# Seven of twelve modulation slabs moved from TensorE to VectorE dot products, and the layer loop written out on three engines

## The chip, the core and the metric

The kernel runs on one core of one Trainium2 chip. The metric is the device time of one execution in microseconds (us): the median over the runs shown, lower is better. All times inside an execution are microseconds from the start of the span that the profile shows.

## What is computed

Two layers of a hybrid backbone over 384 tokens (256 latent, 128 context) of width 1024, all in float32. The change touches the modulation vectors `mod` and nothing else of the mathematics:

```python
def _layer(x, cond, prm, ctx):
    mod = jax.nn.silu(cond) @ w_mod + b_mod             # w_mod (1024, 6144), two rows of cond
    sh1, sc1, g1, sh2, sc2, g2 = [m[:, None, :] for m in jnp.split(mod, 6, axis=-1)]
    h = _rmsnorm(x, g_mix) * (1 + sc1) + sh1
    ... = _project(h, w_in, ...)                        # four mixers and four sigmoid gates
    x = x + g1 * (jnp.sum(gates * proj, axis=2) @ w_o)
    h2 = _rmsnorm(x, g_ffn) * (1 + sc2) + sh2
    a, b = jnp.split(h2 @ w_gu, 2, axis=-1)
    x = x + g2 * ((jax.nn.silu(a) * b) @ w_down)
```

`mod` has 6144 columns: 24 slabs of 256, or 48 chunks of 128. The kernel holds it as `modc`, 48 columns by two rows of `cond` (latent and context).

## The kernel before

**Units.** All big products are cut into units of 128 output columns by 384 tokens. A unit has K steps of 128 rows (8, or 4 for a `proj` unit, 5 or 6 for `down`), and a step is three matmuls (`product`, L763 to L765), since both operands are split in a high and a low part. So a K=8 unit is 24 matmuls and a K=4 unit 12. A slot of a unit on ScalarE (`slot`, then `split`) copies the high part of the weights of the unit three places on (`w_hi`, L1078, LOOKAHEAD = 3); VectorE subtracts for the low part (`w_lo`, L1329). TensorE waits for `lo_ready` of its unit. The raw weights come from SyncE's queue into a ring of four slabs (two units each).

**Order.** Nothing is scheduled at run time: `plan()` writes a table `HOOKS` that says after which unit each small step runs, and every engine walks the same table. One layer is: norm, q, k, v units; conv and pool units with attention woven in; 32 gate and proj units of the first two branches; then the stage of this change, 32 more units from N_AC on (four times four `gate` units of K=8 and four `proj` units of K=4), numbered here slot 0 to 31; then 8 `out` units from N_O on, of which the first three run as `three_units`, which first waits for `lo_ready` of all three; then norm 2, 44 feed-forward units (an inner hardware loop of four turns over 8 units, `pe.Fori(0, 4)`), and 32 `down` units.

**A proj slot on VectorE** is: low part of the unit three on, then the hooks, then the product with the gate (`gate_t`, L1377, waits for the unit's end). GpSimd adds the product into `merged` (L1773), ScalarE and VectorE split `merged` into `br_hi` and `br_lo` for the out units.

**Modulation.** Slabs of layer 0: eight at the start; slabs 8 to 19 in the 32 slots of the stage of this change (`mod` after slots 2, 4, ... 12 and 18, 20, ... 28); slabs 20 to 23 ("late") before norm 2. Each of the twelve is three hooks: `load` (ScalarE's queue, 1 MB into `mod_w`), `mod` (TensorE, eight matmuls of 256 columns, `mod_matmul` L834, then a copy of the sums by ScalarE), `sel` (TensorE, two transposes, `mod_turn` L840, then two small VectorE instructions, `mod_columns`). Layer 1 gets its columns another way: during layer 0's feed-forward and down units `dot_next` makes 34 chunks as VectorE dot products (two instructions of 128x1024 elements per chunk, L1440, one per row of `cond`, and after every second chunk one small combination, L1447); three slabs ("tail") and four late ones stay on TensorE.

**The layer loop.** `with pe.Fori(0, DEPTH) as l` (L988), and the same on the four other engines, is a hardware loop: the code of a layer stands once and a backward branch repeats it. Everything that only layer 0 does stands in `engine.If(l < DEPTH - 1)`.

Of the kernel before, what the change touches and what calls it, by code (L numbers as in the profile page):

```python
# [26 lines left out]
P = 128  # L27
# [6 lines left out]
DEPTH = 2  # L34
D = 1024
# [77 lines left out]
DOTS = 34  # L113
AHEAD = ("load", "mod", "sel", "cond_next", "load_next", "dot_next", "load_tail_next")

NA = 20
# [10 lines left out]
def plan():  # L128
# [123 lines left out]
    return units, slab_of, hooks, mid, base, last_unit  # L252

UNITS, SLABS, HOOKS, MID, BASE, LAST_UNIT = plan()
# [76 lines left out]
def program(nc, io, sizes):  # L332
    with ExitStack() as ctx:
# [134 lines left out]
        mod_in = [signal(f"mod_in{s}", 0, step=32) for s in range(2)]  # L468
# [169 lines left out]
        def mod_index(i, it):  # L638

            return i + it * 6  # L640

# [6 lines left out]
        def run_hooks(engine, l, n, it, hook, takes, mid):  # L648

            hooks = mid + HOOKS[n]
            for what, i in hooks:
# [102 lines left out]
        def _(pe):  # L755
# [93 lines left out]
            def hook(l, what, i, it):  # L849
                if what == "mod":  # L850
                    f, slot = mod_index(i, it), i % 2
                    pe.wait_ge(*mod_in[slot](0, i // 2 + it * 3))
                    if i >= 2:
                        pe.wait_ge(*mod_ready(0, f - 2))
                    mod_matmul(sc[:, slot, :], mod_w[:, slot, :], mod_sum.sem)
                elif what == "sel":
                    pe.wait_ge(*mod_row_ready(0, mod_index(i, it)))
# [130 lines left out]
            with pe.Fori(0, DEPTH) as l:  # L988
# [53 lines left out]
                with pe.If(l < DEPTH - 1):  # L1042
# [27 lines left out]
        def _(act):  # L1070
# [74 lines left out]
            def hook(l, what, i, it):  # L1145
                if what == "load":
                    f, slot = mod_index(i, it), i % 2
                    if i < 2:
                        act.wait_ge(*attn_ready(l, NA - 1))
                    if i >= 2:  # L1150
                        act.wait_ge(*mod_sum(0, f - 2))
                    load_mod(act, mod_w[:, slot, :], l, bass.ds(8 + i + it * 6, 1), mod_in[slot].sem)
                elif what == "load_late":
                    act.wait_ge(*unit_done(l, N_O - 1))
                    load_mod(act, late_w[i], l, slice(20 + i, 21 + i), late_in[i].sem)
                elif what == "mod":
                    f = mod_index(i, it)
                    act.wait_ge(*mod_sum(0, f))
                    if i >= 2:
                        act.wait_ge(*mod_col(0, f - 2))  # L1160
# [5 lines left out]
                elif what == "load_next":  # L1166

                    j = i + it * 4
                    if i >= 2:
                        act.wait_ge(*dot_both(0, j - 2))  # L1170
# [76 lines left out]
            def slot(l, n, it=0, per=0):  # L1247

                if n + LOOKAHEAD >= U:
                    with act.If(l < DEPTH - 1):  # L1250
# [3 lines left out]
                run_hooks(act, l, n, it, hook, ("load", "mod", "cond_next", "load_next", "load_tail_next"), MID[n])  # L1254
                post(l, n, it, per)
# [30 lines left out]
            with act.Fori(0, DEPTH) as l:  # L1286
# [21 lines left out]
                with act.If(l < DEPTH - 1):  # L1308
# [12 lines left out]
        def _(dve):  # L1321
# [103 lines left out]
            def hook(l, what, i, it):  # L1425
                if what == "sel":
                    dve.wait_ge(*mod_col(0, mod_index(i, it)))
                    c = 16 + 2 * i + it * 12
                    mod_columns(bass.ds(c, 2), sc[:, i % 2, :], i % 2, vec[:, bass.ds(c, 2)],
                                mod_added(0, mod_index(i, it)), mod_ready.sem)  # L1430
                elif what == "dot_next":
                    j = i + it * 4
                    if i == 0:
                        dve.wait_ge(*cond_in(0, 0))
                    dve.wait_ge(*dot_in[i % 2](0, i // 2 + it * 2))
                    if i % 2 == 0:
                        dve.wait_ge(*dot_ready(0, i // 2 + it * 2 - 1))
# [6 lines left out]
                    if i % 2:  # L1444
                        c = bass.ds(j - 1, 2) if i < 4 else slice(i - 1, i + 1)
                        b = vec_all[:, bass.ds((l + 1) % DEPTH, 1), c].rearrange("p a v -> p (a v)")
# [117 lines left out]
            def norm(l, which, start=None):  # L1564
# [30 lines left out]
                if which:  # L1595
                    dve.wait_ge(*mod_ready(0, 11))
                    gains(0, DC, tail_ready(l, -1), 4)
                for d in range(DC + 1):
                    if which == 0 and d % 2 == 0 and d < DC:
# [4 lines left out]
                        gains(d, 2, start_ready(0, d + 1) if start else dot_ready(0, DOTS // 2 - 1), d // 2)  # L1604
# [9 lines left out]
            def slot(l, n, it=0, per=0):  # L1614
# [4 lines left out]
                if n + LOOKAHEAD >= U:  # L1619
                    with dve.If(l < DEPTH - 1):  # L1620
# [3 lines left out]
                run_hooks(dve, l, n, it, hook, ("sel", "dot_next"), MID[n])  # L1624
# [58 lines left out]
            with dve.Fori(0, DEPTH) as l:  # L1683
                chain.enter("layer", l)
# [25 lines left out]
                with dve.If(l < DEPTH - 1):  # L1710
# [8 lines left out]
                chain.leave(DEPTH)  # L1719
# [134 lines left out]
```

## Time and profile before

| what | value |
|---|---|
| median of 3 runs | 1471.04 us (1470.63 to 1473.37) |
| profiled execution, own time | 1470.59 us |
| its span | 1468.8 us |
| PE busy | 1435.2 us (98%) |
| DVE busy | 873.0 us (59%) |
| ACT busy | 591.6 us (40%) |
| POOL busy | 179.0 us (12%) |
| HBM read | 211.98 MB, 146 GB/s over the span |

PE is TensorE, PEld its weight loads, DVE VectorE, ACT ScalarE, POOL GpSimd. The own time is 1.79 us more than the span. A matmul's duration is longer than the distance to the next one, since they are pipelined; costs on TensorE are read from start to start.

### The profile page before, as it was taken

Reading aid. Unit: us, or ns where it says so; the run is one execution under the profiler, and the core shown is the slowest. Engines: PE = TensorE matmul, PEld = TensorE weight load, DVE = VectorE, ACT = ScalarE, POOL = GpSimd, SP = SyncE. Lnnn points to the kernel's source line nnn. Section 1 sums busy time; section 2 is a strip of 40 time slices with the busy share of each in tenths; the row PEclk is TensorE's granted clock in tenths of the full one; section 3 lists DMA queues with packets and bytes.
Section 4 is the critical chain, followed back from the end, with each engine's and each line's share of the span. In section 5 each row is a group of like instructions: output and inputs, shape, how many; then the busy total and the mean of one; then the engine's idle time right before and its main releaser. Section 6 shows DMA issues by size and latency. Waiting matters only on the chain.

```text
span 1468.8 us, 25970 instructions
## 1 busy us (share of the span) xinstructions
PE 1435.2 (98%) x9053; PEld 1376.1 (94%) x9053; DVE 873.0 (59%) x1609; ACT 591.6 (40%) x1082; POOL 179.0 (12%) x173
## 2 busy tenths in 40 slices
PE   5999999999999999999999999999999999999998
PEld 4899999998989999999988999999999989999998
DVE  4776666553454877777876766655444574545333
ACT  3544545442343533332344544554333353333322
POOL 2220020111222000000102211101131300000000
PEclk7999999999999999999999999999999999999999
DMA  9532123346566555546844321232343733433341
GB/s 346 189 122 88 58 87 96 107 154 234 193 224 229 194 179 190 195 157 212 282 139 131 122 87 58 93 110 87 108 151 117 257 105 127 142 114 101 107 133 49
DMA packets 68371, 215.69 MB, mean 147 GB/s; under 512 B 7896, under 2 KB 9240, under 8 KB 68120
## 3 DMA queue, kind: packets, MB, share of 16 engines
q1 hardware_dynamic: 55736, 168.50, 34.2%
q10 hardware_dynamic: 12096, 44.57, 8.7%
q8 instruction: 69, 1.13, 0.3%
q0 software_dynamic: 416, 1.05, 0.2%
q14 instruction: 54, 0.44, 0.1%
HBM read 211.98 MB, written 2.11 MB: 146 GB/s over the span
## 4 chain that ended last, share of the span: by engine, by line
PE 93%; DVE 2%; issue 2%; DMA 1%; ACT 1%; POOL 0%; ACTq 0%; DVEq 0%; POOLq 0%
PE bank L763 29%; PE bank L764 28%; PE bank L765 28%; PE tr L932 2%; PE sc L908 2%; PE tr L917 2%; DMA mod_w<-in_w_mod_pack 1%; PE sc L834 1%; PE tr L864 1%; DMA tok<-in_x_prompt 0%; DVE w_lo L1329 0%; DVE nx L1581 0%; PE bank L941 0%; ACT h_hi L1241 0%; PE bank L834 0%
## 5 line engine op out<-in xcount | busy, mean ns | idle before, releaser
L763 PE MATMUL bank<-h_hi,w_lo 128*128 128x384 f32 x1664 | 568.6, 342 | 10.2 <-DVE h_lo L1334 7.6
L765 PE MATMUL bank<-h_hi,w_hi 128*128 128x384 f32 x1664 | 558.1, 335 | 0.0
L764 PE MATMUL bank<-h_lo,w_hi 128*128 128x384 f32 x1664 | 558.1, 335 | 0.0
L1329 DVE TENSOR_TENSOR w_lo<-raw,w_hi 128x1024 fp32r<-128x1024 f32 (+3 forms) x352 | 384.0, 1092 | 284.0 <-ACT w_hi L1078 283.8
L1078 ACT CAST w_hi<-raw 128x1024 fp32r<-128x1024 f32 (+3 forms) x352 | 323.6, 922 | 126.2 <-PE bank L765 104.1
L763 PEld LDWEIGHTS bank<-h_hi,w_lo 128*128 128x128 f32 x1664 | 313.8, 189 | 22.9 <-issue 15.2
L764 PEld LDWEIGHTS bank<-h_lo,w_hi 128*128 128x128 f32 x1664 | 314.1, 189 | 0.0
L765 PEld LDWEIGHTS bank<-h_hi,w_hi 128*128 128x128 f32 x1664 | 313.8, 189 | 0.0
L763 PE MATMUL bank<-br_hi,w_lo 128*128 128x384 f32 x384 | 131.9, 343 | 1.5 <-DVE w_lo L1329 1.5
L765 PE MATMUL bank<-br_hi,w_hi 128*128 128x384 f32 x384 | 128.6, 335 | 0.0
L764 PE MATMUL bank<-br_lo,w_hi 128*128 128x384 f32 x384 | 128.4, 334 | 0.0
L765 PE MATMUL bank<-f_hi,w_hi 128*128 128x384 f32 x352 | 117.6, 334 | 0.0
L763 PE MATMUL bank<-f_hi,w_lo 128*128 128x384 f32 x352 | 117.6, 334 | 0.0
L764 PE MATMUL bank<-f_lo,w_hi 128*128 128x384 f32 x352 | 117.6, 334 | 0.0
L1773 POOL TENSOR_TENSOR merged<-merged,gate_t 128x384 f32<-128x384 f32 x48 | 69.6, 1458 | 385.8 <-DVE gate_t L1377 385.8
L1201 ACT ACTIVATE prob<-sc,st,q_rs 128x384 f32<-128x384 f32 (+1 forms) x96 | 56.6, 596 | 100.5 <-DVE st L1520 50.3
L1440 DVE SCALAR_TENSOR_TENSOR unread<-mod_t,cond_all 128x1024 bf16<-128x1024 f32 x68 | 85.3, 1254 | 1.2
L763 PEld LDWEIGHTS bank<-br_hi,w_lo 128*128 128x128 f32 x384 | 72.1, 188 | 6.8 <-issue 6.8
L1090 ACT ACTIVATE f_hi<-ff_f 128x384 f32 (+1 forms) x44 | 23.1, 526 | 137.0 <-DVE ff_f L1361 137.0
L764 PEld LDWEIGHTS bank<-br_lo,w_hi 128*128 128x128 f32 x384 | 72.2, 188 | 0.0
L765 PEld LDWEIGHTS bank<-br_hi,w_hi 128*128 128x128 f32 x384 | 72.1, 188 | 0.0
L763 PEld LDWEIGHTS bank<-f_hi,w_lo 128*128 128x128 f32 x352 | 66.1, 188 | 0.0
(191 smaller groups left out, 1295.2 us busy)
## 6 DMA issues: line engine op xcount, KB each, us to landing
raw<-in_w_pack SPq DMA_DIRECT2D x224, 512.0 KB, 4.5
mod_t<-in_w_mod_t ACTq DMA_DIRECT2D x34, 512.0 KB, 3.8
raw<-in_w_pack SPq DMA_DIRECT2D x64, 256.0 KB, 3.3
mod_w<-in_w_mod_pack ACTq DMA_DIRECT2D x32, 512.0 KB, 5.0
raw<-in_w_pack SPq DMA_DIRECT2D x32, 384.0 KB, 4.0
raw<-in_w_pack SPq DMA_DIRECT2D x32, 320.0 KB, 3.5
start_w<-in_w_mod_pack SPq DMA_DIRECT2D x12, 512.0 KB, 12.8
late_w<-in_w_mod_pack ACTq DMA_DIRECT2D x8, 512.0 KB, 12.1
```

What stands on the lines that cost most here:

```text
L763: pe.matmul(out, w[1], r[0], start=start, stop=False)
L764: pe.matmul(out, w[0], r[1], start=False, stop=False)
L765: return pe.matmul(out, w[0], r[0], start=False, stop=stop)
L908: ins = pe.matmul(sc[:, g, nk * n:nk * n + nk], q_[a, 4 * m + c, P * t:P * t + P], k_[a, ks], start=r == 0, stop=r == 2)
L917: ins = pe.transpose(tr[:, g, P * b:P * b + P], prob[:, i % 2, g, P * b:P * b + P], ident)
L932: ins = pe.matmul(tr[64 * g:64 * g + 64, 0, to], vals[:, m, v, 64 * g:64 * g + 64], prob_t[:, i % 2, g, b + n, :], start=b == 0, stop=v == ...
L1078: act.copy(to, src).then_inc(hi_ready.sem, 1)
L1090: act.mul(f_hi[:, c, :].rearrange("p a t -> p (a t)"), ff_f[:, i % 2, :], 0.5).then_inc(ff_hi.sem, 1)
L1201: ins = act.activation(prob[:, i % 2, g, nk * n:nk * n + nk], sc[:, g, nk * n:nk * n + nk], ACT.Exp, scale=q_rs[:, 2 + 4 * m + c, r:r + 1] ...
L1329: dve.tensor_tensor(to, src, hi.bitcast(F32), ALU.subtract).then_inc(lo_ready.sem, 1)
L1440: dve.scalar_tensor_tensor(unread[:, :], mod_t[:, i % 2, :], 1.0, cond_all[:, c, :], ALU.mult, ALU.mult, accum_out=dot_sums[:, i % 2, c:c ...
L1773: pool.tensor_tensor(m, m, gate_t[:, d % 4, :], ALU.add).then_inc(merge_done.sem, 1)
```

## The change

In layer 0's stage from N_AC on, slabs 8 to 12 stay on TensorE (each now through the single buffer `tail_w`, `load` at slot 6x, `mod` at 6x + 4, `sel` at 6x + 5), and slabs 13 to 19 become 14 chunks that VectorE computes as dot products, at slots 3, 5, ... 29 (`dot_gate`). Their weights come as 512 KB chunks (`load_gate`), after one load of the condition rows to all partitions (`cond_gate`, 1 MB). TensorE, ScalarE and VectorE run the two layers as written-out code; the inner feed-forward loops, and the layer loops of SyncE and GpSimd, stay.

```diff
-AHEAD = ("load", "mod", "sel", "cond_next", "load_next", "dot_next", "load_tail_next")
+GATE_SLABS, GATE_DOTS = 5, 14
+AHEAD = ("cond_gate", "load_gate", "dot_gate", "load", "mod", "sel", "cond_next", "load_next", "dot_next", "load_tail_next")
...
-    for x, at in enumerate((2, 4, 6, 8, 10, 12)):
-        hooks[AC + at - 2].insert(0, ("load", x))
-        hooks[AC + at].append(("mod", x))
-        hooks[AC + at + 1].insert(0, ("sel", x))
+    gate_stage(0, "cond_gate", 0)
+    for x in range(2):
+        gate_stage(0, "load_gate", x)
+    for x in range(GATE_DOTS):
+        gate_stage(3 + 2 * x, "dot_gate", x)
+        if x + 2 < GATE_DOTS:
+            gate_stage(4 + 2 * x, "load_gate", x + 2)
+    for x in range(GATE_SLABS):
+        gate_stage(6 * x, "load", x)
+        gate_stage(6 * x + 4, "mod", x)
+        gate_stage(6 * x + 5, "sel", x)
...
             if following:
-                with engine.If(l < DEPTH - 1):
+                if l < DEPTH - 1:
...
-            with pe.Fori(0, DEPTH) as l:
+            for l in range(DEPTH):
...
+                elif what == "cond_gate":
+                    act.wait_ge(*attn_ready(l, NA - 1))
+                    act.wait_ge(*kv_stored(l, 0))
+                    act.dma_start(cond_all[:, :, :].rearrange("p c k -> p (c k)"),
+                                  cond_row.rearrange("c k -> (c k)").unsqueeze(0).broadcast_to([P, 2 * D])).then_inc(cond_in.sem, 16)
+                elif what == "load_gate":
+                    if i >= 2:
+                        act.wait_ge(*dot_both(0, i - 2))
+                    chunk = 16 + 2 * GATE_SLABS + i
+                    load_chunk(act, mod_t[:, i % 2, :], l, slice(chunk, chunk + 1), dot_in[i % 2].sem)
...
-            with act.Fori(0, DEPTH) as l:
+            for l in range(DEPTH):
...
-                elif what == "dot_next":
+                elif what in ("dot_gate", "dot_next"):
...
                 if which:
-                    dve.wait_ge(*mod_ready(0, 11))
+                    dve.wait_ge(*mod_ready(0, GATE_SLABS - 1))
+                    dve.wait_ge(*dot_ready(0, GATE_DOTS // 2 - 1))
...
-            with dve.Fori(0, DEPTH) as l:
+            for l in range(DEPTH):
```

Two places in the order of instructions. First VectorE at the end of the stage, before, from the split of slot 29 (for the first out unit) to the split of slot 30: `w_lo` is the low part of a later unit, `gate_t` a proj product, `mod_sums` and `modc` the `sel` of a slab, `br_lo` the split of `merged`.

```order
L1329 TENSOR_TENSOR w_lo<-raw,w_hi 128x1024 [waits hi_ready]
L657 COMPARE_AND_BRANCH
L1420 TENSOR_REDUCE mod_sums<-sc 128x4 [waits mod_col]
L1422 TENSOR_TENSOR modc<-mod_sums,vec 128x4 [waits mod_added]
L657 UNCONDITIONAL_BRANCH
L1371 REGISTER_ALU
L1372 REGISTER_ALU [waits unit_done]
L1377 SCALAR_TENSOR_TENSOR gate_t<-gate_t,bank 128x384 [waits gate_ready]
L1329 TENSOR_TENSOR w_lo<-raw,w_hi 128x1024 [waits hi_ready]
```

The same place in the changed kernel (lines 21 higher), from the same split in slot 29 to the split of slot 30:

```order
L1350 TENSOR_TENSOR w_lo<-raw,w_hi 128x1024 [waits hi_ready]
L1462 SCALAR_TENSOR_TENSOR unread,mod_sums<-mod_t,cond_all 128x1024 [waits dot_both,dot_in1]
L1462 SCALAR_TENSOR_TENSOR unread,mod_sums<-mod_t,cond_all 128x1024 [waits dot_first]
L1473 SCALAR_TENSOR_TENSOR modc<-mod_sums,vec 128x4 [waits dot_both]
L1441 TENSOR_REDUCE mod_sums<-sc 128x4 [waits mod_col]
L1443 TENSOR_TENSOR modc<-mod_sums,vec 128x4 [waits mod_added]
L1398 SCALAR_TENSOR_TENSOR gate_t<-gate_t,bank 128x384 [waits gate_ready,unit_done]
L1350 TENSOR_TENSOR w_lo<-raw,w_hi 128x1024 [waits hi_ready]
```

The last dot (two long instructions and a small one) now stands between the split of slot 29 and everything behind it.

Second, TensorE at the end of a layer, before: the last matmuls of `three_units` for the next layer's first units, and the backward branch.

```order
L763 MATMUL bank<-h_hi,w_lo 128x384
L764 MATMUL bank<-h_lo,w_hi 128x384
L765 MATMUL bank<-h_hi,w_hi 128x384
L1042 UNCONDITIONAL_BRANCH
L988 REGISTER_ALU
L988 COMPARE_AND_BRANCH
```

The same place in the changed kernel (lines 11 higher), with the first matmuls of unit 3 of layer 1 behind it:

```order
L774 MATMUL bank<-h_hi,w_lo 128x384
L775 MATMUL bank<-h_lo,w_hi 128x384
L776 MATMUL bank<-h_hi,w_hi 128x384
L774 MATMUL bank<-h_hi,w_lo 128x384 [waits lo_ready]
L775 MATMUL bank<-h_lo,w_hi 128x384
```

The branches and the register step are gone, and unit 3 follows directly.

## Rows read from the trace of the kernel before

**Rows 1.** The page: busy time of TensorE, and the granted clock in 40 slices.

```profile
PE 1435.2 (98%) x9053; PEld 1376.1 (94%) x9053; DVE 873.0 (59%) x1609; ACT 591.6 (40%) x1082; POOL 179.0 (12%) x173
PEclk7999999999999999999999999999999999999999
```

**Rows 2.** Timeline of TensorE in layer 0: start, duration, operation; one slab's `mod`, `sel`.

```profile
330.92 0.34 PE L765 MATMUL bank<-h_hi,w_hi 128*128 128x384 f32 x1
...
332.18 0.44 PE L763 MATMUL bank<-h_hi,w_lo 128*128 128x384 f32 x1
332.46 0.34 PE L764 MATMUL bank<-h_lo,w_hi 128*128 128x384 f32 x1
...
336.28 0.34 PE L765 MATMUL bank<-h_hi,w_hi 128*128 128x384 f32 x1
336.59 0.42 PE L763 MATMUL bank<-br_hi,w_lo 128*128 128x384 f32 x1
336.85 0.34 PE L764 MATMUL bank<-br_lo,w_hi 128*128 128x384 f32 x1
```

**Rows 3.** Timeline of TensorE: first and last matmul of the stage, both layers.

```profile
318.61 0.33 PE L763 MATMUL bank<-h_hi,w_lo 128*128 128x384 f32 x1
436.23 0.34 PE L765 MATMUL bank<-br_hi,w_hi 128*128 128x384 f32 x1
437.60 0.44 PE L763 MATMUL bank<-br_hi,w_lo 128*128 128x384 f32 x1 [1.03 <-DVE w_lo L1329]
...
1043.61 0.33 PE L763 MATMUL bank<-h_hi,w_lo 128*128 128x384 f32 x1
1143.27 0.34 PE L765 MATMUL bank<-br_hi,w_hi 128*128 128x384 f32 x1
```

**Rows 4.** Timeline of VectorE in the feed-forward stage: one dot of an odd chunk.

```profile
507.64 1.22 DVE L1440 SCALAR_TENSOR_TENSOR unread<-mod_t,cond_all 128x1024 bf16<-128x1024 f32 x1
510.78 0.56 DVE L1361 TENSOR_TENSOR ff_f<-ff_s,bank 128x384 f32<-128x384 f32 x1
```

**Rows 5.** Windows (busy us and count of each engine, clock, DMA): stage, feed-forward.

```profile
318.60:436.40 117.80, 117.36 (x793) 106.64 (x792) 46.02 (x77) 38.60 (x66) 22.46 (x17) 1.00 0.64 225
486.00:620.00 134.00, 134.00 (x775) 133.91 (x774) 106.63 (x167) 50.91 (x71) 0.00 (x0) 1.00 0.58 199
```

**Rows 6.** DMA issues: KB each, median us from issue to landing.

```profile
mod_t<-in_w_mod_t ACTq DMA_DIRECT2D x34, 512.0 KB, 3.8
```

**Rows 7.** Timeline of VectorE at the end of the stage in layer 0.

```profile
431.30 1.23 DVE L1329 TENSOR_TENSOR w_lo<-raw,w_hi 128x1024 fp32r<-128x1024 f32 x1 [1.74 <-ACT w_hi L1078]
...
433.30 1.22 DVE L1329 TENSOR_TENSOR w_lo<-raw,w_hi 128x1024 fp32r<-128x1024 f32 x1
434.61 0.56 DVE L1377 SCALAR_TENSOR_TENSOR gate_t<-gate_t,bank 128x384 f32<-128x384 f32 x1
435.61 1.86 DVE L1329 TENSOR_TENSOR w_lo<-raw,w_hi 128x1024 fp32r<-128x1024 f32 x1 [0.44 <-ACT w_hi L1078]
```

**Rows 8.** Timeline of TensorE: from `three_units` to the step behind unit 3.

```profile
55.07 0.33 PE L765 MATMUL bank<-h_hi,w_hi 128*128 128x384 f32 x1
...
59.40 0.72 PE L864 MATMUL tr<-const,q_sq 128*128 128x2 f32 x6
...
775.87 0.34 PE L765 MATMUL bank<-h_hi,w_hi 128*128 128x384 f32 x1
778.57 0.44 PE L763 MATMUL bank<-h_hi,w_lo 128*128 128x384 f32 x1 [2.36 <-issue]
...
784.40 0.72 PE L864 MATMUL tr<-const,q_sq 128*128 128x2 f32 x6
```

**Rows 9.** Windows, and a row of TensorE's timeline: waits and the clock.

```profile
757.00:763.00 6.00, 4.05 (x37) 3.15 (x38) 4.31 (x14) 2.34 (x5) 0.87 (x1) 1.00 0.19 77
779.00:783.00 4.00, 4.00 (x16) 4.00 (x15) 2.25 (x2) 1.03 (x2) 0.00 (x0) 0.57 0.23 85
...
761.57 0.45 PE L763 MATMUL bank<-h_hi,w_lo 128*128 128x384 f32 x1 [1.74 <-DVE h_lo L1334]
```

More of the change, by code:

```diff
@@ L251, in plan @@
         last_unit[u["slab"]] = n
-    return units, slab_of, hooks, mid, base, last_unit
-UNITS, SLABS, HOOKS, MID, BASE, LAST_UNIT = plan()
+    return units, slab_of, hooks, mid, base, last_unit, gate_hooks
+UNITS, SLABS, HOOKS, MID, BASE, LAST_UNIT, GATE_HOOKS = plan()
 U, S = len(UNITS), len(SLABS)
@@ L467, in program @@
         start_in = [signal(f"start_in{s}", 0, step=32) for s in range(6)]
-        mod_in = [signal(f"mod_in{s}", 0, step=32) for s in range(2)]
+        mod_in = signal("mod_in", 0, step=32)
         late_in = [signal(f"late_in{s}", 1, step=32) for s in range(4)]
@@ L651, in run_hooks @@
             hooks = mid + HOOKS[n]
+            if N_AC <= n < N_AC + 16:
+                hooks = hooks + GATE_HOOKS.get((n, it), [])
             for what, i in hooks:
@@ L1041, in _ @@
                     unit(l, n)
-                with pe.If(l < DEPTH - 1):
+                if l < DEPTH - 1:
                     def tail(x):
@@ L1253, in slot @@
                     split(l, n + LOOKAHEAD, it, per)
-                run_hooks(act, l, n, it, hook, ("load", "mod", "cond_next", "load_next", "load_tail_next"), MID[n])
+                run_hooks(act, l, n, it, hook, ("cond_gate", "load_gate", "load", "mod", "cond_next", "load_next", "load_tail_next"), MID[n])
                 post(l, n, it, per)
@@ L1307, in _ @@
                     slot(l, n)
-                with act.If(l < DEPTH - 1):
+                if l < DEPTH - 1:
                     for j in range(3):
@@ L1444, in hook @@
                     if i % 2:
-                        c = bass.ds(j - 1, 2) if i < 4 else slice(i - 1, i + 1)
-                        b = vec_all[:, bass.ds((l + 1) % DEPTH, 1), c].rearrange("p a v -> p (a v)")
+                        if gate:
+                            c = slice(15 + 2 * GATE_SLABS + i, 17 + 2 * GATE_SLABS + i)
+                            b = vec[:, c]
+                        else:
+                            c = bass.ds(i + it * 4 - 1, 2) if i < 4 else slice(i - 1, i + 1)
+                            b = vec_all[:, bass.ds((l + 1) % DEPTH, 1), c].rearrange("p a v -> p (a v)")
                         dve.scalar_tensor_tensor(modc[:, c, :], dot_sums[:, :, :], 0.5,
@@ L1603, in norm @@
                                 start(d // 2)
-                        gains(d, 2, start_ready(0, d + 1) if start else dot_ready(0, DOTS // 2 - 1), d // 2)
+                        gains(d, 2, start_ready(0, d + 1) if start else dot_ready(0, (GATE_DOTS + DOTS) // 2 - 1), d // 2)
                     if d == 0:
@@ L1708, in _ @@
                     slot(l, n)
-                with dve.If(l < DEPTH - 1):
+                if l < DEPTH - 1:
                     mean_square(l + 1, 0)
```

56 lines of the change are left out of this document (28 added, 28 removed).

## The prediction

> **What bounds the kernel now.** I read the page first: TensorE is busy 98% of the span, and its clock is granted in full in every slice but the first [rows 1]. So time is won only where TensorE does less work or waits less. Then I read TensorE's timeline around the places that the change touches, start to start. A matmul of 384 columns follows the one before after about 0.17 us at full clock, so a K=8 unit takes 4.17 us (24 steps) and a K=4 unit 2.08 us. The other engines matter only where TensorE waits for them; for that I read three joints: the stage with the twelve slabs, its end, and the backward branch between the layers.
>
> **The twelve slabs on TensorE.** In layer 0 the stage runs from 318.61 to 436.23, in layer 1, which does no modulation there, from 1043.61 to 1143.27 [rows 3]: 117.62 against 99.66 us, so the twelve slabs cost 17.96 us. One of them in detail: the `mod` step opens a gap of 332.18 - 330.92 - 0.17 = 1.09 us, and the matmul after it is followed 0.28 us later instead of 0.17, which makes 1.20; `sel` takes 336.59 - 336.28 - 0.17 = 0.14 and 0.09 behind it [rows 2], 0.23. That is 1.43 us for a slab, 17.2 for twelve; the remaining 0.8 us are waits for `mod_w` (512 KB halves asked for only two slots ahead). After the change five slabs remain, 7.15 us, and `load` is four slots ahead of `mod`, at least 8.3 us and mostly 14, so I put the waits at nothing. **Saved in the stage: 17.96 - 7.15 = 10.8 us.** The bounds: 10.0 if the waits stay, 10.8 otherwise.
>
> **What the dots cost VectorE.** An odd chunk in the feed-forward stage takes from 507.64 to 510.78 [rows 4], 3.14 us with the small combination behind it; an even one lacks that, so 14 of them take at most 44 us. VectorE is busy 46.0 of 117.8 us in the stage now. With the stage down to 107 us it would be at most 90 of 107, 84%. In the feed-forward stage the same engine is busy 106.63 of 134.00 us, 80%, with a dot in every second slot, and TensorE is busy in all 134.00 of them [rows 5]. So on the average the dots are hidden; what counts is how they are bunched. A stretch of four proj units is 8.3 us of TensorE. VectorE has there three K=8 splits at 1.2 us and a K=4 one (half, by its elements), four products at 0.56, and two dots at 3.1 or less: 12.6 us, so it falls up to 4.3 us behind. But a split is made three units ahead, and behind the stretch come four gate units, 16.7 us, with some 10 us of VectorE work. The split that suffers most is due three K=8 units later, 12.5 us, against some 2.3 us for ScalarE's and its own pass and the 4.3 of arrears. TensorE doesn't wait. The same holds for three of the four proj stretches.
>
> **The fourth stretch is the end of the stage,** and there no slack follows: `three_units` wants the low parts of three K=8 units at once, the last of which is split in slot 31, when TensorE has one proj unit left. TensorE waits there already: 437.60 - 436.23 = 1.37 us from start to start, 1.2 more than the usual distance [rows 3]. VectorE's chain up to it is [rows 7]: split at 431.30, (sel and product), split at 433.30, product at 434.61, split at 435.61, which lasts 1.86. The order shows the last dot (slot 29, an odd one) between the first of these and all the others. Its 3.14 us move the chain back, less what the chain idles now: 434.61 - 433.30 - 1.22 = 0.09 and 435.61 - 434.61 - 0.56 = 0.44, in all 0.5. **Cost 2.6 us, taken as 2.5**, since pitches are a little under durations. Bounds: 1.8 if the last split then takes 1.22 us as the others do (it was slow, 1.86, beside GpSimd's merges), and 4.5 if two of the three splits and the dot meet the merges, at 0.64 each. Queued behind that dot are the products of slots 29 to 31, so the merges and `br_lo` of the last four chunks come 2.5 us later; TensorE wants chunk 4 only after 36 matmuls, 6.3 us, and it starts 2.5 us later itself, so this costs nothing.
>
> **The wait and the clock.** The wait grows to 1.37 + 2.5 = 3.9 us from start to start. The trace has two neighbours. After a wait of 1.74 us at 761.57 the clock stays at its upper level (1.00 granted, 2.4 GHz); after 2.36 us at 778.57 it falls, 0.57 granted from 779 to 783, mostly the 1.2 GHz level [rows 8, 9]. At 3.9 us I take the fall, at the price of that place. The Trainium skill (TensorE: Matmul & The Clock Gate, Part 1) has the clock halved after TensorE was idle, in windows that run freely whatever the kernel does; by it the fall is likely here but may come late or not at all, and the sum would be 1.6 us lower without it, which is the first rival.
>
> **The layer loop.** In layer 0 the step behind unit 3 starts 59.40 - 55.07 = 4.33 us after the last matmul of `three_units`; in layer 1, with the backward branch between, 784.40 - 775.87 = 8.53 us [rows 8]. **That is 4.2 us, all of it gone if the gap is the branch's:** 2.6 us of standing still, "issue" in the profile, so no engine is waited for, and 1.6 us of the lower clock behind it. The straight code of layer 0 shows no such gap anywhere, so written-out code of the same density should feed TensorE as well. The price of the clock after a wait, 1.6 us, is from here too. What else was behind `If` and registers costs nothing on TensorE: the stage in layer 1, with all its skipped hooks, is 576 matmuls in 99.66 us, 0.173 each.
>
> **Transfers.** Twelve slabs of 1 MB become five, 14 chunks of 512 KB and 1 MB of condition rows: the same traffic. A chunk lands in 3.8 us [rows 6] and is asked for three slots ahead; ScalarE waits for a dot before it asks for the next chunk, which may hold its own split back by a microsecond or so, within the three units of lead. Should chunks be late, the cost is bounded by what a late dot costs: nothing before slot 29, and there 1 us for 1 us.
>
> **Sum.** -10.8 (slabs) + 2.5 (end of the stage) + 1.6 (clock) - 4.2 (branch) = -10.9 us. Against the profiled execution's own time, 1470.59, that is 1459.7. The median of the runs is 0.45 higher than that execution, so I forecast **1460.1 us**, 0.7% faster.
>
> **Rivals.**
> - *The clock stays up at the end of the stage.* For it: 1.74 us did nothing. 1458.5 us. Chance 0.25.
> - *VectorE is behind in the earlier proj stretches too*, because dots and merges slow each other (a split took 1.86 instead of 1.22 us once per such stretch). It takes over 5 us of arrears beyond my 4.3 before TensorE waits; then each stretch costs some 1 to 4 us, with the clock. Against it: the averages. 1463 to 1470 us. Chance 0.14.
> - *The gap at the layer joint is not the branch's* but that of a fresh stretch of code for three engines at once; it stays. 1464.3 us. Chance 0.07.
> - *Slower: the inner loops' backward branches begin to stall.* Their code lies elsewhere in the written-out program. There are three backward branches in each layer's feed-forward stage on TensorE; today none shows, the window of 134.00 us there is busy throughout [rows 5]. 
> - *A bit better still:* the last dot is absorbed, no growth of the wait, 1456 us. Chance 0.05.
>
> **How the numbers follow.** The likeliest case has 0.45, its rival without the clock 0.25. The bounds of the end of the stage (1.8 to 4.5) and of the waits (0.8) give 1458.6 to 1463 around the likeliest; with the second, third and last rivals the range of 8 in 10 is 1456.5 to 1465.5. About 0.2%, 2.9 us, is what a measurement of this kernel can tell from no change. Faster than 1468.1: all but the upper end of the second rival and the slower one, 0.90. Within 0.2%: 0.06. Slower: 0.04.
>
> **What would show it.** The stage in layer 0 should run from first to last matmul in about 107 us. The first matmul of the out units should stand some 3.9 us behind the last proj one, waiting for `w_lo`, and the window behind it should show a granted clock under 1.00. VectorE's busy time in the stage should be near 85 us. At the layer joint unit 3 should follow at 0.17 us, and the window after it be at 1.00. I am wrong if TensorE waits for `w_lo` inside the stage, if the joint still shows "issue", or if the feed-forward windows are no longer filled.

## The result, and the profile after

The changed kernel takes **1460.39 us** (median of 5 runs, 1458.47 to 1463.97) against 1470.69 us for the kernel before (5 runs); the ratio is 0.9932, 95% interval 0.9917 to 0.9946. The forecast was 1460.1 us. The profiled execution's own time is 1458.97 us with a span of 1457.0, so 11.6 us less than the one of before. That total hides one term that came out smaller, one that did not fall due in this execution, and one that I had not seen.

The page of the changed kernel (lines of TensorE's code stand 11 higher, of VectorE's 21 higher or more) answers to [rows 1]: TensorE is as busy as before, VectorE's 14 new dots are 28 more passes.

```profile
PE 1422.4 (98%) x8927; PEld 1370.1 (94%) x8927; DVE 909.2 (62%) x1658; ACT 589.7 (40%) x1075; POOL 177.3 (12%) x173
PEclk7999999999999999999999999999999999999999
L1462 DVE SCALAR_TENSOR_TENSOR unread<-mod_t,cond_all 128x1024 bf16<-128x1024 f32 x96 | 122.1, 1272 | 1.7
```

TensorE's timeline at a fixed step of the start, at the stage's first and last matmul and behind it in layer 0, at the end of layer 1's stage, and at the last transposes (start, duration, instruction, idle time before it). The inner five answer to [rows 3]:

```profile
42.32 0.44 PE L851 MATMUL bank<-const,next_row 128*128 128x128 f32 x2 [1.82 <-ACT next_row L1299]
...
318.89 0.33 PE L774 MATMUL bank<-h_hi,w_lo 128*128 128x384 f32 x1
425.78 0.34 PE L776 MATMUL bank<-br_hi,w_hi 128*128 128x384 f32 x1
428.77 0.41 PE L774 MATMUL bank<-br_hi,w_lo 128*128 128x384 f32 x1 [2.66 <-DVE w_lo L1350]
...
1130.47 0.34 PE L776 MATMUL bank<-br_hi,w_hi 128*128 128x384 f32 x1
1132.24 0.41 PE L774 MATMUL bank<-br_hi,w_lo 128*128 128x384 f32 x1 [1.43 <-DVE w_lo L1350]
...
1449.61 0.66 PE L1074 MATMUL bank<-const,x 128*128 128x128 f32 x4 [0.83 <-DVE x L1365]
```

The stage in layer 0 lasts 425.78 - 318.89 = 106.89 us instead of 117.62. The wait behind it is 2.99 us from start to start instead of 1.37. In layer 1, where no dot runs, the same wait grew too: 1.77 us instead of 0.77.

Windows of the stage, of the first 4 us behind its end, and of the layer joint (length, busy us of PE, PEld, DVE, ACT and POOL, granted clock, DMA share, GB/s), to be read against [rows 5] and [rows 9]:

```profile
318.60:426.00 107.40, 107.40 (x669) 102.85 (x667) 80.21 (x125) 36.14 (x58) 23.17 (x16) 1.00 0.74 254
428.70:432.70 4.00, 3.93 (x23) 3.96 (x24) 3.82 (x6) 1.99 (x3) 1.97 (x2) 1.00 0.75 256
765.00:771.00 6.00, 6.00 (x36) 6.00 (x36) 4.65 (x10) 4.40 (x8) 0.43 (x1) 1.00 0.70 232
```

TensorE waits for nothing inside the stage, VectorE is busy 80.2 us of it, and the clock is 1.00 behind the wait. At the joint the timeline of TensorE runs on at once, which answers to [rows 8]:

```profile
767.27 0.33 PE L776 MATMUL bank<-h_hi,w_hi 128*128 128x384 f32 x1
767.44 0.33 PE L774 MATMUL bank<-h_hi,w_lo 128*128 128x384 f32 x1
771.60 0.72 PE L874 MATMUL tr<-const,q_sq 128*128 128x2 f32 x6
```

VectorE's timeline at the end of layer 0's stage answers to [rows 7]:

```profile
420.86 1.23 DVE L1350 TENSOR_TENSOR w_lo<-raw,w_hi 128x1024 fp32r<-128x1024 f32 x1 [1.83 <-ACT w_hi L1088]
422.00 1.22 DVE L1462 SCALAR_TENSOR_TENSOR unread<-mod_t,cond_all 128x1024 bf16<-128x1024 f32 x1
...
425.36 1.22 DVE L1350 TENSOR_TENSOR w_lo<-raw,w_hi 128x1024 fp32r<-128x1024 f32 x1
426.50 0.55 DVE L1398 SCALAR_TENSOR_TENSOR gate_t<-gate_t,bank 128x384 f32<-128x384 f32 x1
426.96 1.55 DVE L1350 TENSOR_TENSOR w_lo<-raw,w_hi 128x1024 fp32r<-128x1024 f32 x1
```

**The balance of the two profiled executions,** from anchors on TensorE: the stage starts 0.28 us later (318.89 against 318.61; the step at 42.32 stands at 42.03 before, so this is the program's start); the stage -10.73; its end wait 2.99 - 1.37 = +1.62; the joint -4.20 (4.33 us from 767.27 to 771.60, as in layer 0, where it was 8.53); layer 1's end wait +1.00. Sum -12.0; the own times differ by 11.6. Of the remaining 0.4, half lies in three stretches of other work, less than 0.1 each, and half outside the span.

### The profile page after: what moved, and what is told of

Same layout as the page of the kernel before. It is cut to its first block, busy times and chain, and to the rows that moved or that the text cites. A ratio compares the mean times of both kernels' runs of the same rounds, so it can differ in the third digit from the quotient of the medians.

```text
span 1457.0 us, 24014 instructions
## 1 busy us (share of the span) xinstructions
PE 1422.4 (98%) x8927; PEld 1370.1 (94%) x8927; DVE 909.2 (62%) x1658; ACT 589.7 (40%) x1075; POOL 177.3 (12%) x173
## 4 chain that ended last, share of the span: by engine, by line
PE 94%; DVE 2%; issue 2%; ACT 1%; DMA 0%; POOL 0%; ACTq 0%; POOLq 0%; DVEq 0%
PE bank L774 29%; PE bank L776 28%; PE bank L775 28%; PE tr L942 2%; PE sc L918 2%; PE tr L927 2%; PE tr L874 1%; PE sc L845 1%; DVE w_lo L1350 1%; DMA tok<-in_x_prompt 0%; DVE nx L1607 0%; PE bank L951 0%; ACT h_hi L1262 0%; DVE h_lo L1355 0%; DVE nf L1612 0%
## 5 line engine op out<-in xcount | busy, mean ns | idle before, releaser
L1350 DVE TENSOR_TENSOR w_lo<-raw,w_hi 128x1024 fp32r<-128x1024 f32 (+3 forms) x352 | 388.1, 1103 | 249.8 <-ACT w_hi L1088 249.5
L1462 DVE SCALAR_TENSOR_TENSOR unread<-mod_t,cond_all 128x1024 bf16<-128x1024 f32 x96 | 122.1, 1272 | 1.7
L1136 ACT ACTIVATE gate_t<-bank 128x384 f32<-128x384 f32 x64 | 31.6, 494 | 94.1 <-PE bank L776 85.1
```

What stands on the lines that cost most here:

```text
L1136: act.activation(gate_t[:, i % 4, :], ps, ACT.Tanh, scale=0.5).then_inc(gate_ready.sem, 1)
L1350: dve.tensor_tensor(to, src, hi.bitcast(F32), ALU.subtract).then_inc(lo_ready.sem, 1)
L1462: dve.scalar_tensor_tensor(unread[:, :], mod_t[:, i % 2, :], 1.0, cond_all[:, c, :], ALU.mult, ALU.mult, accum_out=dot_sums[:, i % 2, c:c ...
```

## The experiments

All were run beside the kernel before. "Corrected" times below run from TensorE's step at 42.32 us to its last transposes at 1449.61, 1407.29 us in the changed kernel. They leave out the start of the program: that step stands at 41.4 to 44.5 us in these profiles. The clock seems to have a share in that: over the window from 20 to 36 us the granted clock is 0.63 in the changed kernel's profile and 0.50 in those of experiments 3 and 4, which start latest. The intervals of the medians are about 2 us wide to either side, so differences of 1 or 2 us between experiments are read from the profiled executions, one for each kernel.

**1. Only the written-out layers.** The kernel before, with this edit on TensorE, ScalarE and VectorE:

```diff
-            with pe.Fori(0, DEPTH) as l:
+            for l in range(DEPTH):
...
-                with engine.If(l < DEPTH - 1):
+                if l < DEPTH - 1:
```

> The kernel before, with the layer loops of TensorE, ScalarE and VectorE written out and nothing else; all twelve slabs stay on TensorE. If the 4.2 us at the layer joint are the branch's: 1470.6 - 4.2 = 1466.4 us own time, unit 3 of layer 1 follows the last matmul of the three units at 0.17 us. If the gap closed for another reason (work that the dots moved): 1470.6 us. The second question is the wait at the end of layer 1's stage, 0.77 us from start to start before and 1.77 after the change, though layer 1 has no dots there. If the written-out code brought it (the engines leave out their skipped hooks, and the last split meets a GpSimd merge), it is near 1.8 here too, and the sum is 1467.4; if the dots did, 0.8.

Measured: 1467.71 us (11 runs, ratio 0.9977, interval 0.9968 to 0.9985), about the 1467.4 of the second case. The joint runs on at 0.17 us. The end wait of layer 0's stage is 1.52 us, that of layer 1's 1.76:

```profile
1139.39 0.34 PE L765 MATMUL bank<-br_hi,w_hi 128*128 128x384 f32 x1
1141.15 0.41 PE L763 MATMUL bank<-br_hi,w_lo 128*128 128x384 f32 x1 [1.43 <-DVE w_lo L1329]
```

Corrected, 1415.99 us against 1419.38 before (42.03 to 1461.41): 3.4 less. So the 1.0 us in layer 1 is a side effect of the written-out code and has nothing to do with the dots.

**2. The change with all three layer loops kept** (`Fori` and `If` back; seven slabs still dots).

> The changed kernel, with the layer loops of all three engines as hardware loops again; seven slabs are still dots. Branch theory: 4.2 us more than the changed kernel, 1459.0 + 4.2 = 1463.2 us, with 2.6 us of standing still and the lower clock behind it at the joint. Rival (the joint's gap does not come from the loop): 1459.0. The stage of layer 0 should take 106.9 us from first to last matmul and its end wait 3.0 us as in the changed kernel. If the written-out code causes the 1.0 us more at the end of layer 1's stage, the wait there is 0.8 again and the time 1462.2.

Measured: 1464.25 us (6 runs, ratio 0.9949, interval 0.9936 to 0.9962). The stage takes 106.9 us, its end wait 2.97, the joint shows the gap again, layer 1's end wait is 0.76. What I had not expected is the clock behind layer 0's stage:

```profile
428.71 0.69 PE L778 MATMUL bank<-br_hi,w_lo 128*128 128x384 f32 x1 [2.63 <-DVE w_lo L1354]
473.15 0.45 PE L778 MATMUL bank<-h_hi,w_lo 128*128 128x384 f32 x1 [1.01 <-DVE h_lo L1359]
...
772.54 0.47 PE L778 MATMUL bank<-h_hi,w_lo 128*128 128x384 f32 x1 [2.42 <-issue]
```

```profile
428.70:432.70 4.00, 3.99 (x12) 3.99 (x13) 3.83 (x6) 1.98 (x3) 2.02 (x2) 0.50 0.72 241
```

From 428.71 to 473.15 are 44.44 us; the changed kernel, with the same wait, needed 470.45 - 428.77 = 41.68 for the same work. The granted clock of 0.50 (the 1.2 GHz level) took 2.8 us there, and nothing in the changed kernel's profile. Corrected, this kernel takes 1413.14 us, 5.9 more than the changed one: 4.3 at the joint (8.61 us instead of 4.33) and 2.8 here, less 1.0 in layer 1.

**3. Only TensorE's layer loop kept.**

> The changed kernel, with TensorE's layer loop alone as a hardware loop again; ScalarE and VectorE stay written out. If the gap at the joint is TensorE's own branch: 4.2 us slower than the changed kernel, 1463.2 us. Rival (ScalarE's or VectorE's branch held up the split or the norm that TensorE then waited for, and the profile did not show it): no gap, 1459.0 us.

Measured: 1464.86 us (6 runs, ratio 0.996, interval 0.9948 to 0.9973). TensorE's timeline at the joint:

```profile
770.71 0.34 PE L780 MATMUL bank<-h_hi,w_hi 128*128 128x384 f32 x1
773.24 0.44 PE L778 MATMUL bank<-h_hi,w_lo 128*128 128x384 f32 x1 [2.19 <-DVE w_lo L1354]
...
777.50 0.72 PE L878 MATMUL tr<-const,q_sq 128*128 128x2 f32 x6
```

The gap is TensorE's own: 2.53 us from start to start, although the other two engines run on. The view names `w_lo` as its releaser, but VectorE had begun the next unit's low part at 771.87, so unit 3's was long done. From 773.24 to 777.50 are 4.26 us, full clock; behind the gaps of 2.36 [rows 8] and 2.42 us the clock fell, behind this one of 2.19 it did not. Corrected, the kernel takes 1410.84 us, 3.6 more than the changed one: 2.4 at the joint, 1.3 for a fall of the clock behind the end wait (42.99 us to the next wait in place of 41.68).

**4. The last dot earlier.**

```diff
+GATE_AT = (3, 5, 7, 9, 11, 13, 15, 17, 19, 21, 23, 25, 26, 27)
...
-        gate_stage(3 + 2 * x, "dot_gate", x)
+        gate_stage(GATE_AT[x], "dot_gate", x)
         if x + 2 < GATE_DOTS:
-            gate_stage(4 + 2 * x, "load_gate", x + 2)
+            gate_stage(GATE_AT[x] + 1, "load_gate", x + 2)
```

> The changed kernel, with the last three of the fourteen dots in slots 25, 26 and 27 in place of 25, 27 and 29, so that none stands in the last four slots of the stage. By my step on the end of the stage the dot in slot 29 alone lengthens the wait for the low part: it goes from 3.0 back to about 1.4 us, start to start, 1.6 us less, 1457.4 us. Rival: the merges on GpSimd, not the dot, set it (the last split took 1.55 us): it stays at 3.0 and the time at 1459.0. If the clock falls behind the 3 us wait in some executions of the changed kernel (its five runs lie 5.5 us apart), the runs here lie closer, within 3 us.

Measured: 1459.1 us (5 runs, 1457.04 to 1459.85, ratio 0.992, interval 0.9907 to 0.9933). The end wait is 1.23 us, no fall of the clock behind it, and the corrected time is 1405.51, 1.8 us less. The runs lie within 2.8 us.

**5. TensorE written out, ScalarE's and VectorE's loops kept.**

> The changed kernel, with the layer loops of ScalarE and VectorE as hardware loops again and TensorE's written out. In the run with all loops kept VectorE stood still from 769.87 to 774.55 us, and its split for unit 4 ended at 775.7; unit 4 would be wanted at 774.3 if TensorE had no gap. Theory (VectorE's branch costs too, but later and less): no gap in front of unit 3, one of about 1.4 us in front of unit 4, waiting for w_lo. Rival (TensorE's branch was all of it): no gap at all. The end of layer 1's stage should wait 0.8 us from start to start, not 1.8, if it is ScalarE's and VectorE's written-out code that moved it. Against the changed kernel +1.4 - 1.0 = +0.4 us: 1459.4 us by the theory, 1458.0 by the rival.

Measured: 1460.92 us (6 runs, ratio 0.9934, interval 0.992 to 0.9949). VectorE at the joint:

```profile
767.14 0.16 DVE L1447 TENSOR_TENSOR modc<-mod_sums,vec 128x4 f32<-128x4 f32 x1
772.05 3.50 DVE L1354 TENSOR_TENSOR w_lo<-raw,w_hi 128x1024 fp32r<-128x1024 f32 x3 [4.74 <-ACT w_hi L1092]
```

and TensorE there and at the end of layer 1's stage:

```profile
773.33 0.45 PE L778 MATMUL bank<-h_hi,w_lo 128*128 128x384 f32 x1 [0.69 <-DVE w_lo L1354]
...
1132.40 0.41 PE L778 MATMUL bank<-br_hi,w_lo 128*128 128x384 f32 x1 [0.55 <-DVE w_lo L1354]
```

VectorE stands still for 4.7 us where the written-out kernel loses 1.1, and the first of the three splits behind it is the one for unit 4. The view names ScalarE's `w_hi` as its releaser, but ScalarE began that copy at 767.29 and ran on without a gap, as in the changed kernel (767.35), so the standing still is VectorE's own. Unit 4 starts 0.96 us behind the instruction ahead of it where the changed kernel has 0.03: TensorE pays 0.9 us, 0.7 of them shown as idle, not the 1.4 that I had put. Layer 1's end wait is 0.89 us: ScalarE's and VectorE's code, not TensorE's, moved it. The corrected time is 1407.41, 0.1 more than the changed kernel's.

**6. The changed kernel once more.**

> The changed kernel once more, for the clock behind the 2.66 us of idle time at the end of layer 0's stage. It stayed up in the profile of the changed kernel, but fell in two others with the same wait, and cost 2.8 and 1.3 us there (from there to the next stage's first wait 44.44 and 42.99 us in place of 41.68). If the fall comes in some executions and not in others, the times scatter from 1458.5 to about 1462 and the median lies 1 to 2 us above the lowest; the profiled run shows 41.7, or up to 44.5. Rival (the clock always stays up in this kernel, and the scatter is from the start of the program): 41.7 us, and the slow executions have a late start.

Measured: 1461.37 us (5 runs, 1459.3 to 1463.12). The profiled run starts like the first one (the step of 42.32 stands at 42.40), but behind the same wait the clock falls for a while:

```profile
428.86 0.41 PE L774 MATMUL bank<-br_hi,w_lo 128*128 128x384 f32 x1 [2.65 <-DVE w_lo L1350]
472.14 0.41 PE L774 MATMUL bank<-h_hi,w_lo 128*128 128x384 f32 x1 [1.10 <-DVE h_lo L1355]
754.55 0.66 PE L774 MATMUL bank<-h_hi,w_lo 128*128 128x384 f32 x1 [1.89 <-DVE h_lo L1355]
```

```profile
428.80:436.80 8.00, 7.94 (x37) 7.97 (x38) 4.54 (x6) 1.98 (x3) 1.96 (x2) 0.79 0.82 257
...
754.50:758.00 3.50, 3.45 (x11) 3.48 (x12) 3.38 (x10) 1.89 (x5) 0.00 (x0) 0.53 0.00 0
```

43.28 us instead of 41.68: 1.6 us, and the corrected time is 1408.87, 1.6 more. So the fall does come in some executions; the start scatters too (44.5 in experiments 3 and 4), but made no difference here. The clock also fell behind the wait of 1.89 us in norm 1 of layer 1, and that cost nothing (from there to layer 1's end wait 379.36 us, 379.35 in the changed kernel's profile, where it stayed up behind the same wait). TensorE waits for VectorE's `h_lo` in that stretch anyway, which would explain it.

**7. Two more passes in the last dot.**

> The changed kernel, with two more passes of VectorE in the last dot (slot 29), 2.5 us. By my step on the end of the stage what is put there comes out at TensorE one for one: wait 3.0 + 2.5 = 5.5 us from start to start. If a longer wait makes the clock fall in every execution, the cost is 2.5 + 1.6 to 2.8: 1463.1 to 1464.3 us, and the runs scatter less than those of the changed kernel. If the clock falls by chance as before: 1461.5 to 1464.3, as wide a scatter.

Measured: 1463.17 us (5 runs, 1462.79 to 1464.24, ratio 0.9948, interval 0.9936 to 0.9961).

```profile
430.37 0.66 PE L776 MATMUL bank<-br_hi,w_lo 128*128 128x384 f32 x1 [5.18 <-DVE w_lo L1352]
474.61 0.41 PE L776 MATMUL bank<-h_hi,w_lo 128*128 128x384 f32 x1 [1.11 <-DVE h_lo L1357]
```

The wait is 5.18 us instead of 2.66: 2.52 for 2.5, one for one. The fall costs 44.24 - 41.68 = 2.6 us, the corrected time is 5.1 us more, and the runs lie within 1.5 us of each other: a long wait costs every time what a short one costs sometimes.

**8. The merge held until the last low part is made.**

```diff
-                with pool.Fori(0, 2) as it:
+                for it in range(2):
                     for i in range(8, 16):
+                        if it == 1 and i == 14:
+                            pool.wait_ge(*lo_ready(l, N_O + 2))
                         merge(l, i, it)
```

> The changed kernel, with GpSimd's merge of slot 30 held until the last low part (unit 34) is made, in both layers. Theory: the last split is slow where it meets a merge (2.08 us in layer 1, 1.55 in layer 0, 1.22 alone); it takes 1.22 in both, and the waits get shorter by 0.86 and 0.33: 1.2 us less, 1457.8 us. Rival (what it meets is something else, a transfer say): 2.08 and 1.55 stay, 1459.0 us. Should the later merges be missed by TensorE, the out units would wait for br_lo; they are wanted 6 us later, so I expect no such wait.

Measured: 1460.25 us (5 runs, ratio 0.9926, interval 0.9913 to 0.9939; the changed kernel beside it 1461.37). In layer 1 the split that took 2.08 us (at 1129.90 in the changed kernel) takes 1.23, and TensorE's wait falls from 1.77 to 0.91. VectorE and GpSimd there, and in layer 0:

```profile
428.21 1.55 DVE L1350 TENSOR_TENSOR w_lo<-raw,w_hi 128x1024 fp32r<-128x1024 f32 x1
...
1132.54 1.23 DVE L1350 TENSOR_TENSOR w_lo<-raw,w_hi 128x1024 fp32r<-128x1024 f32 x1 [0.39 <-ACT w_hi L1088]
```

```profile
426.77 1.91 POOL L1798 TENSOR_TENSOR merged<-merged,gate_t 128x384 f32<-128x384 f32 x1 [5.41 <-DVE gate_t L1398]
430.01 2.29 POOL L1798 TENSOR_TENSOR merged<-merged,gate_t 128x384 f32<-128x384 f32 x2 [1.33 <-DVE w_lo L1350]
```

Right for layer 1, wrong for layer 0: its last split still takes 1.55 us, since it meets the merge of slot 29 (426.77 to 428.68), which I had not held. The corrected time is 1407.82, 0.5 more than the changed kernel's: behind layer 0's wait the clock fell (43.08 us instead of 41.68), which outweighs the 0.9 won in layer 1. The Trainium skill (SBUF — State Buffer, Who interferes with whom) says that a VectorE instruction with two inputs in SBUF contends with a GpSimd one that reads there, and that the order of issue decides which of the two is held up. The 1.23 against 2.08 us agree with the first, and rows further below with the second.

**9. Three passes in every dot,** the third with a result that goes nowhere.

> The changed kernel, with a third pass of VectorE in each of the fourteen dots, 1.25 us each, whose result goes nowhere: 17.5 us more, VectorE busy 80 + 17.5 = 97.5 of 107 us in layer 0's stage. The prediction has VectorE at most 4.3 us behind at the end of a stretch of proj units and 5 more before TensorE waits; here it is 2 x 1.25 = 2.5 us further behind. Theory: no waits inside the stage, 106.9 us from first to last matmul; only the end wait grows by 1.25 (slot 29) or by up to 2.5 if the arrears of slot 27's pass reach it: 1460.2 to 1461.5 us. Rival (VectorE has no such room): gaps for w_lo inside the stage, 3 us or more in all.

Measured: 1469.67 us (11 runs, ratio 1.0005, interval 0.9996 to 1.0014): the whole gain is gone. From 319.03 to 432.77 the stage takes 113.7 us, 6.9 more, and the end wait is 5.03 (4.70 shown as idle). TensorE's long waits inside the stage:

```profile
383.54 0.44 PE L853 MATMUL sc<-const,mod_row 128*128 128x128 f32 x2 [1.55 <-ACT mod_row L1184]
404.89 0.69 PE L853 MATMUL sc<-const,mod_row 128*128 128x128 f32 x2 [3.03 <-ACT mod_row L1184]
```

and ScalarE ahead of the second one (ACTq is its queue of DMA issues):

```profile
404.03 0.33 ACTq L676 DMA_DIRECT2D mod_t<-in_w_mod_t  x1
404.46 0.37 ACT L1184 COPY mod_row<-sc 128x256 f32<-128x256 f32 x1 [5.04 <-DVE unread L1469]
```

Both my theory and its rival are wrong on the way: TensorE waits neither for nothing nor for `w_lo`. ScalarE may ask for a chunk only when the dot two before it is done; the copy of a slab's sums (`mod_row`) stands behind that wait in the same queue, and TensorE's `sel` waits for the copy. This holds TensorE at two of the five slabs, the third and the fourth; at the second, ScalarE's copy comes late without a cost. The two waits are 4.6 of the 6.9 us. Most of the rest is the clock, which fell behind the second (0.63 granted over 404.90 to 408.90).

**10. Four passes in every dot.**

> As the run with three passes, with four passes in each dot: 35 us more on VectorE, 115 us of work in a stage of 107. VectorE must fall behind for good: the stage from first to last matmul is at least 115 us plus what VectorE waits, 118 to 124 us, and the time 1459 + 11 to 17 + the clock's losses: 1470 to 1482 us. If the time stays below 1465, VectorE's work was not what bounds a denser stage.

Measured: 1485.89 us (4 runs, ratio 1.0108, interval 1.0092 to 1.0123). The end wait is 8.75 us, three waits for `mod_row` of 1.86, 4.11 and 5.59 us and one for `w_lo` of 1.28 stand inside the stage, and the granted clock over it is 0.95. The median is 3.9 us above my upper end.

**11. Both remedies,** the dots of 4 and the merge of 8.

> The changed kernel, with both remedies: the last three dots in slots 25, 26 and 27, and the merge of slot 30 held behind the last split. End wait of layer 0 about 1.2 us from start to start less up to 0.3, that of layer 1 0.9 in place of 1.77: against the changed kernel 1.8 + 0.9 = 2.7 us less, 1456.3 us at equal start. No clock fall behind either wait. If the two remedies are the same one (the dot's delay only made the split meet the merge), 1457.4 us.

Measured: **1455.9 us** (4 runs, 1455.59 to 1457.48), ratio 0.9911 to the kernel before, interval 0.9895 to 0.9926. TensorE's two end waits:

```profile
426.58 0.41 PE L775 MATMUL bank<-br_hi,w_lo 128*128 128x384 f32 x1 [0.72 <-DVE w_lo L1351]
...
1129.13 0.41 PE L775 MATMUL bank<-br_hi,w_lo 128*128 128x384 f32 x1 [0.58 <-DVE w_lo L1351]
```

1.06 and 0.91 us from start to start; the corrected time is 1404.42, 2.9 less than the changed kernel's, 2.7 were forecast.

**12. Nine slabs as 18 dots,** with both remedies.

```diff
-GATE_SLABS, GATE_DOTS = 5, 14
+GATE_SLABS, GATE_DOTS = 3, 18
+GATE_AT = (3, 5, 7, 8, 9, 10, 11, 13, 15, 16, 17, 18, 19, 21, 24, 25, 26, 27)
```

> As the kernel with both remedies, and two more slabs as dots: nine of twelve, 18 dots in the slots 3, 5, 7 to 11, 13, 15 to 19, 21, 24 to 27, three slabs on TensorE. Each slab takes 1.43 us from TensorE, so 2.9 us less than with both remedies, 1453.5 us, if VectorE (busy 80 + 4 x 2.5 = 90 of 104 us) and the chunks (3.5 us each, asked for one slot ahead at the densest) keep up. Rival (a chunk is late or VectorE is behind in the dense stretches): gaps for w_lo in the stage, more than 2.9 us of them if it is no gain at all.

Measured: 1456.57 us (4 runs, ratio 0.991, interval 0.9895 to 0.9925), no better than experiment 11. The stage is shorter, 104.72 us, but VectorE, which has no idle time from 396 us on, makes the split of slot 28 at 420.62, when TensorE has 2.8 us of the stage left, and TensorE pays behind the stage:

```profile
420.62 0.68 DVE L1351 TENSOR_TENSOR w_lo<-raw,w_hi 128x512 fp32r<-128x512 f32 x1
...
425.24 1.55 DVE L1351 TENSOR_TENSOR w_lo<-raw,w_hi 128x1024 fp32r<-128x1024 f32 x1
```

```profile
427.05 0.66 PE L775 MATMUL bank<-br_hi,w_lo 128*128 128x384 f32 x1 [3.31 <-DVE w_lo L1351]
471.54 0.41 PE L775 MATMUL bank<-h_hi,w_lo 128*128 128x384 f32 x1 [1.10 <-DVE h_lo L1356]
```

The wait of 3.66 us from start to start is 2.6 more than in experiment 11, and the clock's fall behind it costs 44.49 - 41.68 = 2.8; by the corrected time, 1407.76, this execution is 3.3 us slower than that of experiment 11. (-2.2 in the stage, +2.6, +2.8.)

## Why the prediction was right, and where it was not

**The slabs, -10.8: right.** Measured -10.73, and the transfers' waits (0.8) are gone as assumed.

**The end of the stage, +2.5: right in mechanism, 0.9 too large.** The split behind the last dot stands 4.50 us after the one ahead of it (420.86, 425.36) instead of 2.00 [rows 7]: 2.5 us later, for a dot whose two passes and combination took 2.6 us from 422.00 on and not 3.14. Behind it the chain gave back 0.7 us, where I had counted 0.5, and the last split took 1.55 us instead of 1.86. What comes out is +1.62. I had taken the other splits' 1.22 only as a bound; below the bound of 1.8 the case lies because the dot was too dear: the 3.14 us from [rows 4] is the distance from one start to a later one, and holds 0.37 us in front of the combination and 0.10 behind it in which VectorE runs nothing. It also put VectorE's work in the stage too high: near 85 us were forecast, 80.2 were measured. Experiments 4 and 7 show that this dot makes the growth of the wait: without it 1.23 us, with two more passes 5.52.

**The clock, +1.6: a matter of chance, and I had put it as a fact with a rival.** In the profiled execution it stayed at 1.00, as the first rival has it; that rival's 1458.5 us is close to the own time of 1458.97. Six profiles have nearly the same wait, 2.53 to 2.77 us idle: from there to the next stage's first wait it took 41.68, 41.71, 42.99, 43.08, 43.28 and 44.44 us. So the fall cost 0, 0, 1.3, 1.4, 1.6 and 2.8 us. Behind the waits of 3.31, 4.70, 5.18 and 8.41 us it came every time (1.9 to 2.8 us), behind those of 1.18 us and less at this place never. The mean of the six, 1.2 us, is close to the 1.6 taken. The median of the runs lies 1.4 us above the profiled one, but that shows nothing about this fall, since the program's start alone scatters by more. The neighbour that I had taken as a sign that the clock stays up, the wait of 1.74 us in norm 1 of layer 1 [rows 9], shows no more than chance either: behind the same 1.74 us it fell in experiment 2, and over all 14 profiles (1.74 to 1.90 us of idle time there) it fell in seven. The Trainium skill (TensorE: Matmul & The Clock Gate, Part 1) has the clock decided in windows that run freely, whatever the kernel does, so that it depends on where in them the work lies; that the same wait brings the fall in one execution and not in the next agrees with that.

**The layer loop, -4.2: right.** The joint gave back exactly that. Experiment 3 shows that 2.4 us of it are TensorE's own branch whatever the other engines do, and the rest the clock's, which fell in two of the three profiles with that gap. So this term too was in part chance: with the clock up in the kernel before, the joint would have given back some 2.5 us. VectorE's branch is longer (4.7 us of standing still against 1.1), but lies behind splits made ahead and costs TensorE 0.9 us.

**Missed: +1.0 at the end of layer 1's stage.** I had said that what stood behind `If` costs nothing. On TensorE that holds; with ScalarE and VectorE written out things shifted a little: the last split begins 0.93 us behind the product ahead of it (1128.97, 1129.90) instead of 0.78, meets the merge which that product started, and takes 2.08 us instead of 1.25. The split and that merge, before and after:

```profile
1142.65 1.25 DVE L1329 TENSOR_TENSOR w_lo<-raw,w_hi 128x1024 fp32r<-128x1024 f32 x1 [0.24 <-ACT w_hi L1078]
1142.79 1.98 POOL L1773 TENSOR_TENSOR merged<-merged,gate_t 128x384 f32<-128x384 f32 x1
...
1129.90 2.08 DVE L1350 TENSOR_TENSOR w_lo<-raw,w_hi 128x1024 fp32r<-128x1024 f32 x1 [0.39 <-ACT w_hi L1088]
1129.89 1.01 POOL L1798 TENSOR_TENSOR merged<-merged,gate_t 128x384 f32<-128x384 f32 x1
```

Before, the split begins 0.14 us ahead of the merge and it is the merge that takes twice its time; after, the merge begins 0.01 us ahead and the split pays. Counted from the stage's last matmul, the merge begins 0.10 us earlier than before and the split 0.05 us later. Experiments 1, 2, 3 and 5 place this (1.76 and 1.64 us with those two engines written out, 0.76 and 0.89 with their loops kept), experiment 8 shows the merge as its cause; ScalarE and VectorE were not tried one by one.

The three deviations, 0.9 less, 1.0 more, and the clock's share (1.2 us in the mean of the six instead of 1.6), nearly cancel. That the median lies within 0.3 us of the forecast is luck: the start alone scatters by more, and in the profiled execution, where the whole 1.6 us of the clock did not fall due, the forecast for it was 0.7 too high. In the range's working there is also a slip without weight: its lower end around the likeliest case, 1458.6 us, takes off the 0.8 of the transfers' waits, which the sum had already put at nothing; without that it is 1459.4.

**The room in the earlier stretches, 4.3 us of arrears and over 5 more: the conclusion held, the reason was wrong.** The order of the kernel needs no more than VectorE can do (80.2 of 107 us, no wait inside). But 2.5 us more per stretch (experiment 9) already costs 6.9 us in the stage. I had counted how early a split is due and named ScalarE's wait for a dot only as something that "may hold its own split back"; it also holds the slab's row back, for which TensorE waits. The second rival's chance of 0.14 was for a wait for `w_lo`; the margin that decides is that of ScalarE's queue, and 1.25 us more in each dot uses it up.

Not tried: whether the inner loops' branches would stall with another placement of the code. In the changed kernel no gap stands in the feed-forward stage.

## What to carry to other kernels

Work moved to an idle engine costs what it delays at the places where another engine waits without slack. Look for the last of the moved pieces and put it elsewhere: here two edits of a few lines took 2.9 us more off, by the profiled executions, a quarter of what the whole change brought, while two more slabs on the same engine brought nothing. When one queue both asks for the next transfer and carries a copy that a third engine needs, the room is that queue's, not the busy engine's; adding work on purpose finds it at once. And a profile of one execution can show a clock fall or not: compare the same stretch in several before giving it a price.

## What the runs showed of the hardware

- The start of the program scatters by 3 us (41.4 to 44.5 for the same step), so times of single executions are compared from that step on. The two latest starts had 0.50 granted from 20 to 36 us, the changed kernel's profile 0.63.
- The clock's fall behind an idle TensorE is neither certain nor excluded between 1.7 and 2.8 us of idle time: it came behind 1.74 (experiment 2), 1.89 (0.53 granted, experiment 6), 2.36, 2.42, 2.53, 2.63, 2.65 and 2.66 (experiment 8), and stayed away behind 1.74 (the kernel before), 1.89, 2.19, 2.66 and 2.77. When it came behind 2.5 us or more it cost 1.3 to 2.8 us; the one behind 1.89 in experiment 6 cost nothing.
- A taken backward branch over a whole layer's code holds TensorE for 2.4 to 2.6 us (experiments 2 and 3, and the kernel before) and VectorE for an estimated 3.6 us (4.7 less 1.1, experiment 5). In ScalarE's timeline there no gap shows.
- A VectorE subtraction of 128x1024 takes 1.22 us alone and 1.55, 1.86 or 2.08 when it begins inside a merge on GpSimd; where it began 0.14 us ahead of the merge it took 1.25 and the merge 1.98 instead of 1.01. In layer 1 a shift of 0.15 us decided.
